# Attention with the value products two units behind, two buffers for the turned probabilities, and the next unit's maxima between a unit's two normalisations

## The reference, cut to what matters

```python
def one_block(qblk):
    s = jnp.einsum('bqhgd,bkhd->bhgqk', qblk, k).astype(jnp.float32) * scale
    p = jax.nn.softmax(s, axis=-1).astype(v.dtype)
    return jnp.einsum('bhgqk,bkhd->bqhgd', p, v)
```

## Time and profile before

| what | value |
|---|---|
| median of 3 runs | 4145.35 us (4144.81 to 4147.48) |
| the profiled execution | 4145.56 us, its trace spans 4143.8 us |
| attention loop in the trace | from scores(0) at 189.85 us to TensorE's restart at 366.76 us |
| mean granted TensorE clock | 0.983 of full speed |

### The profile page before, as it was taken

One profiled execution on the slowest core, in us unless ns is written; L12 is line 12 of the kernel. 1 busy time (PEld: TensorE's weight loads), 2 busy tenths in 40 slices (PEclk: granted clock), 3 DMA queues, 4 the chain that ended last, 5 costly groups with the idle time before them and its releaser, 6 DMA issues.

```text
span 4143.8 us, 57586 instructions
## 1 busy us (share of the span) xinstructions
PE 3886.4 (94%) x21170; PEld 3362.8 (81%) x21170; DVE 2826.8 (68%) x4491; ACT 1696.9 (41%) x2936; POOL 2232.5 (54%) x1240
## 2 busy tenths in 40 slices
PE   7978899999999999999979989999999999999997
PEld 5756898888888888878769989888888888788876
DVE  3774227988875588888863322788887548888886
ACT  3264324556666322222231132455666632222223
POOL 1101234665556677777742323465565667777774
PEclk9999999999999999999999999999999999999998
DMA  5302224778888998898945312477888889988994
GB/s 201 124 1 110 100 99 164 249 269 284 292 299 309 314 307 303 301 314 297 316 147 182 107 57 92 160 243 258 280 300 282 311 312 306 314 295 299 313 316 160
DMA packets 395800, 972.44 MB, mean 235 GB/s; under 512 B 32048, under 2 KB 221232, under 8 KB 381744
## 3 DMA queue, kind: packets, MB, share of 16 engines
q1 hardware_dynamic: 301664, 630.72, 45.2%
q0 software_dynamic: 92160, 335.59, 22.7%
q10 hardware_dynamic: 1744, 3.21, 0.2%
HBM read 835.37 MB, written 133.96 MB: 234 GB/s over the span
## 4 chain that ended last, share of the span: by engine, by line
issue 41%; POOL 34%; PE 17%; DMA 4%; DVE 3%; ACT 1%; POOLq 0%; DVEq 0%; ACTq 0%
POOL SL L444 18%; POOL ROWS L451 14%; PE PS L762 10%; PE PS L564 5%; POOL SL L435 3%; DMA ROWS<-u_exp,EI 2%; DMA ROWS<-v_exp,EI 1%; PE PS L754 1%; DVE ROWS L1267 1%; PE PS L715 1%; DVE OH L1256 0%; DVE PO L1193 0%; ACT SH L995 0%; PE PS L774 0%; DVE TS L1188 0%
## 5 line engine op out<-in xcount | busy, mean ns | idle before, releaser
L444 POOL TENSOR_TENSOR SL<-RW,SH 128x1024 fp32r<-128x1024 f32 x512 | 1284.0, 2508 | 928.6 <-ACT SH L995 887.7
L774 PE MATMUL PS<-WH,SH 128*128 128x480 f32 x2048 | 786.9, 384 | 63.3 <-DVE WL L1317 60.7
L762 PE MATMUL PS<-HH,SH 128*128 128x480 f32 x2048 | 804.5, 393 | 7.8 <-POOL SL L444 6.5
L995 ACT CAST SH<-RW 128x1024 fp32r<-128x1024 f32 x512 | 535.9, 1047 | 613.8 <-PE PS L762 514.1
L762 PE MATMUL PS<-HL,SH 128*128 128x480 f32 x2048 | 780.0, 381 | 0.0
L762 PE MATMUL PS<-HH,SL 128*128 128x480 f32 x2048 | 779.8, 381 | 0.0
L774 PE MATMUL PS<-WH,SL 128*128 128x480 f32 x2048 | 777.2, 379 | 0.0
L774 PE MATMUL PS<-WL,SH 128*128 128x480 f32 x2048 | 776.9, 379 | 0.0
L435 POOL TENSOR_TENSOR SL<-RW,SH 128x1024 fp32r<-128x1024 f32 x84 | 202.5, 2414 | 815.8 <-ACT SH L819 815.8
L1034 ACT CAST WH<-GL 128x480 fp32r<-128x480 f32 x256 | 152.0, 594 | 938.1 <-DVE GL L1311 934.0
L1273 DVE SCALAR_TENSOR_TENSOR ACC<-ROWS,AA,ACC 128x1024 f32<-128x1024 f32 x256 | 399.1, 1559 | 186.8 <-DMA ROWS<-v_exp,EI 174.4
(11 more groups left out here) (171 smaller groups left out, 5358.6 us busy)
## 6 DMA issues: line engine op xcount, KB each, us to landing
RW<-u_blk SPq DMA_DIRECT2D x256, 512.0 KB, 4.3
RW<-v_blk SPq DMA_DIRECT2D x256, 512.0 KB, 5.5
gate_acts<-GE SPq DMA_DIRECT2D x256, 240.0 KB, 2.9
router_weights<-GT SPq DMA_DIRECT2D x60, 1024.0 KB, 4.7
GB<-router_weights SPq DMA_DIRECT2D x32, 1920.0 KB, 12.7
GL<-gate_acts SPq DMA_DIRECT2D x256, 240.0 KB, 4.7
RW<-wstream SPq DMA_DIRECT2D x100, 512.0 KB, 4.5
AW<-wpairs SPq DMA_DIRECT2D x40, 1024.0 KB, 5.2
```

The source lines that it names most:

```text
L444: nc.gpsimd.tensor_tensor(SL[:, r % 2], RW[:, r % RAW], SH[:, r % 2].bitcast(F32), ALU.subtract).then_inc(raw_used, 1)
L762: last = mm(PS[:, n % 2, NG:NS], w[:, n % 2, j], a[:, j, NG:NS], start=(j == 0 and q == 0), stop=(j == DJ - 1 and q == 2))
L774: last = mm(PS[:, dj, NG:NS], w[:, k % 2, dj], a[:, k, NG:NS], start=start, stop=stop)
L995: nc.scalar.copy(SH[:, r % 2], RW[:, r % RAW]).then_inc(hi_done, 1)
```

## The change

Three edits, all in the attention loop:

1. **Order on TensorE and ScalarE.** values runs two units behind instead of one: round n is scores(n+1), values(n-2), turn(n, 0), turn(n, 1). On ScalarE turned(n-1) now stands ahead of out_high(n-2). PT gets a second buffer (in the area WK, which has no other use in this loop), taken in turn.
2. **Order on VectorE.** Round n becomes: normalisation (n, 0), maxima of n+1 (0, 1), normalisation (n, 1), out_low(n-2).
3. RS holds the sums of two units (4 columns instead of 2).

No instruction is added or removed in the loop; only their places and the buffers change.

```diff
-    RS = tiny("RS", 2)
+    RS = tiny("RS", 4)
...
-    PT, _ = sb("PT", [P, 2, NT], F32, at=at_H + 3 * NT * 4)
+    PT = [sb(f"PT{k}", [P, 2, NT], F32, at=at)[0] for k, at in enumerate((at_H + 3 * NT * 4, at_WK))]
...
             if n + 1 < len(UNITS):
                 scores(n + 1)
-            if n > 0:
-                values(n - 1)
+            if n > 1:
+                values(n - 2)
             turn(n, 0)
             turn(n, 1)
+        values(len(UNITS) - 2)
         values(len(UNITS) - 1)
...
+            if n > 0:
+                turned(n - 1)
             if n > 1:
                 out_high(n - 2)
-            if n > 0:
-                turned(n - 1)
+        turned(len(UNITS) - 1)
         out_high(len(UNITS) - 2)
-        turned(len(UNITS) - 1)
         out_high(len(UNITS) - 1)
...
+        def largest(n, half):
+            w = key_tiles(n) * P
+            dve.wait_ge(score_done, 2 * n + half + 1)
+            v.reduce_max(MX[:, half:half + 1], PSf[:, half * 1024:half * 1024 + w], AX_X)
+            dve.drain()
+            v.tensor_scalar(NB[:, half:half + 1], MX[:, half:half + 1], -1.0, None, ALU.mult).then_inc(nb_done, 1)
+
+        def normalised(n, half):
+            dve.wait_ge(exp_done, 2 * n + half + 1)
+            at = 2 * (n % 2) + half
+            v.reciprocal(RI[:, half:half + 1], RS[:, at:at + 1])
+            dve.drain()
+            pr = PR[n % 2][:, half, 0:key_tiles(n) * P]
+            v.tensor_scalar(pr, pr, RI[:, half:half + 1], None, ALU.mult).then_inc(p_done, 1)
+
+        largest(0, 0)
+        largest(0, 1)
         for n in range(len(UNITS)):
-            w = key_tiles(n) * P
-            for half in range(2):
-                dve.wait_ge(score_done, 2 * n + half + 1)
...
+            normalised(n, 0)
+            if n + 1 < len(UNITS):
+                largest(n + 1, 0)
+                largest(n + 1, 1)
+            normalised(n, 1)
             if n > 1:
                 out_low(n - 2)
```

More of the change, by code:

```diff
@@ L685, in values @@
                         val = VC[:, m * P + a:m * P + b]
-                    last = mm(PSf[a:b, 3584:3584 + P], val, PT[:, half, kt * P:(kt + 1) * P],
+                    last = mm(PSf[a:b, 3584:3584 + P], val, PT[n % 2][:, half, kt * P:(kt + 1) * P],
                               start=(kt == 0), stop=(kt == k - 1))
@@ L944, in turned @@
                 act.wait_ge(pt_done, 2 * n + half + 1)
-                nc.scalar.copy(PT[:, half, 0:min(w, NS)],
+                nc.scalar.copy(PT[n % 2][:, half, 0:min(w, NS)],
                                PSf[:, 2048 + half * 512:2048 + half * 512 + min(w, NS)]).then_inc(ptc_done, 1)
             if w > NS:
-                nc.scalar.copy(PT[:, :, NS:NT], PSf[:, 3072:3072 + 2 * P].rearrange("p (h k) -> p h k", h=2)
+                nc.scalar.copy(PT[n % 2][:, :, NS:NT], PSf[:, 3072:3072 + 2 * P].rearrange("p (h k) -> p h k", h=2)
                                ).then_inc(ptc_done, 1)
@@ L957, in _ @@
                 nc.scalar.activation(PR[n % 2][:, half, 0:w], PSf[:, half * 1024:half * 1024 + w], ACT.Exp,
-                                     bias=NB[:, half:half + 1], accum_out=RS[:, half:half + 1]).then_inc(exp_done, 1)
+                                     bias=NB[:, half:half + 1], accum_out=RS[:, 2 * (n % 2) + half:2 * (n % 2) + half + 1]).then_inc(exp_done, 1)
+            if n > 0:
+                turned(n - 1)
             if n > 1:
                 out_high(n - 2)
-            if n > 0:
-                turned(n - 1)
+        turned(len(UNITS) - 1)
         out_high(len(UNITS) - 2)
-        turned(len(UNITS) - 1)
         out_high(len(UNITS) - 1)
@@ L1400, in out_low @@
                             ALU.subtract).then_inc(oh_done, 1)
-        for n in range(len(UNITS)):
-            w = key_tiles(n) * P
-            for half in range(2):
-                dve.wait_ge(score_done, 2 * n + half + 1)
[L1406 to L1415, removed]
+        def largest(n, half):
[13 more added lines that the diff above has]
+        largest(0, 1)
+        for n in range(len(UNITS)):
+            normalised(n, 0)
[3 more added lines that the diff above has]
+            normalised(n, 1)
             if n > 1:
```

## The result

The changed kernel took 4162.02 us (median of 6 runs, 4159.48 to 4166.11), the kernel before 4145.97 beside it; the ratio is 1.0039, with a 95% interval of 1.0027 to 1.0052. That is 16 us slower, above the forecast of +5.9 us and above the range's end of 4159. Slower was forecast, but by +0.14%, less than the 0.2% that I had put as the least to be told from no change.

The account below looks back on a forecast made before the run. The attention loop was taken as bound by a chain of scores, maxima and exponentials (4.37 us a large step). Terms -6.9 + 11.0 + 1.8 = +5.9 on 4145.56 gave 4151.5, less 0.2 for the median 4151.3; range 4147.5 to 4159.

Parts of the forecast that it names:

- Small steps: Seven loop steps of a small unit: no wait for copies, 2.90 against 3.89 us, -0.99 each, -6.9 in all.
- Large steps behind a large unit: 24 loop steps: late second normalisation delays transposes and next scores, 4.83 against 4.37 us, +0.46 each, +11.0 in all.
- Large steps behind a small unit: Seven loop steps: ScalarE's out_high waits for value products of the same step, 4.62 us, +0.25 each, +1.8 in all.
- The end: From scores(39) to TensorE's restart, 8.17 us before: put at no change, within 0.5 us either way.
- The sum at full clock: Total over the attention loop's steps: -6.9 + 11.0 + 1.8 = +5.9 us.
- the fourth rival, the clock: Longer TensorE pause once per group lowers the clock: 1.2 us a step, up to 28 in 24 steps, 4180; chance 0.04.
- Nothing new binds: Rival: large steps stay at 4.37 us and only small steps gain, -6.9 us, 4138.5; chance 0.07.
- Only ScalarE's limit binds: Rival: late transposes cost less, all 31 large steps at 4.62 us, +1.6 us, 4147; chance 0.08.
- The dearer late normalisation: Rival: turn(n, 1) ahead of scores(n+2) in 24 large steps costs 0.61 us each, +10.8 us, 4156; chance 0.13.
- the price of ScalarE's limit: Sum for that rival: 31 x 0.25 - 6.9 = +0.9, about +2.4 with 0.3 a step for rounding; written as +1.6.

Follow-up runs that it names:

- the run with the normalisations first: The changed kernel with both normalisations of n ahead of the maxima of n+1 on VectorE; 4141.41 us, ratio 0.9983.
- the run with the filled pause: The changed kernel plus seven idle matmuls between turn(n, 0) and turn(n, 1) in the round of each group's second unit; 4157.43 us, ratio 1.0022.
- three behind: The changed kernel with out_high and out_low three units behind, and both normalisations ahead of the maxima on VectorE; 4140.22 us, ratio 0.9982.
- the last two kernels: Three behind with the scores by half, 4133.92 us; and the same with one maximum between the normalisations, 4145.25 us.
- scores per half: The kernel before, with scores of half 0 waiting only for its own exponential and issued ahead of half 1; 4137.1 us, ratio 0.9978.
- the kernel three behind with the scores by half: Three behind, with each half's scores waiting only for its own exponential and half 0 issued first; 4133.92 us, ratio 0.9966.

## Why the prediction was wrong

**Small steps:** forecast 2.90, measured 2.93; the gain is 0.96 each, against 0.99 forecast.

**Large steps behind a large unit:** forecast 4.83, measured 4.85. The links are there one by one: the reciprocal directly behind the second NB, the transposes waiting for VectorE, the scores behind them with no wait of their own. That the place of this normalisation is the cause is shown by the run with the normalisations first.

**Large steps behind a small unit:** forecast 4.62, measured 4.52. The value products start at +1.28 when nothing holds them, where I had +1.41 from a row in which they were held for a moment. The exponentials 0.78 apart were right.

**The end:** forecast at no change, measured 8.28 against 8.17.

**The sum at full clock** was thus right: +5.9 forecast, +6.6 measured in the run with the filled pause, +5.6 without the slower start of its trace.

**The step that failed is the fourth rival, the clock.** I named the place (the wait from about +2.4 to +4.2, 1.8 us, once per group, where values belongs to a small unit; measured 1.74) and then gave it a chance of 0.04 and nothing in the sum, with the reason that the clock is 1.00 now with TensorE busy 3.90 of 4.37 us. That row was of the wrong step. The step of the same kind in the kernel before is this one, with the pause of 1.41 us in it:

```profile
281.03:285.40 4.37, 2.96 (x22) 1.96 (x22) 3.48 (x10) 2.25 (x9) 0.00 (x0) 1.00 0.00 0
...
345.47 0.70 PE L657 MATMUL PS<-BIG 64*128 64x512 f32 x2 [1.76 <-ACT PR L957]
```

It has TensorE busy 2.96 of 4.37 us at a clock of 1.00; the changed kernel has 3.12 of 4.85 in its place. So the share there fell only from 0.68 to 0.64, by less than the tenth that I allowed for, and the clock fell behind it all the same. The second row shows that a pause of 1.76 us stood once in the kernel before too, where I had written 1.41 as the longest, and the clock stayed up. What failed is thus the inference from a clock of 1.00 in rows of before to a clock of 1.00 after the change: neither the right row nor the longest pause would have shown that it falls. The runs showed that it does in six of eight groups, in both traces, and not when the pause is filled.

The price was wrong the other way, 28 us for 24 steps: the clock recovers within one step, so a fall costs 1.3 to 1.5 us. The five falls beyond the start cost 6.76 us, and with 2.26 for the slower start (scores(0) to scores(4), 23.46 us against 21.20 in the filled run) that is 9.0 us in all. With 5.9 + 9.0 the forecast would have been 4160.5, in the measured span.

The range ended at 4159 because it left this case out. What stays open is what makes the clock fall. Two groups of eight are spared in each trace, though their pause is the same 1.74 us. The run with the normalisations first had one fall behind a pause of 1.74 us and none behind one of 1.78; three behind had pauses of 1.73 and 1.78 without a fall; and the last two kernels had falls where TensorE had paused for 0.44 us at most in the 6 to 7 us before. So the length of the pause decides nothing alone. Filling it shows, in one trace, only that in the changed kernel the falls do not come without it.

**The other rivals.** Nothing new binds: no; the queues held. Only ScalarE's limit binds: that is the run with the normalisations first, not the change. The dearer late normalisation: no, its links cost what the rows said. In the price of ScalarE's limit one sum of mine does not come out: 0.9 with 0.3 a step for 31 steps is 10.2, and the 2.4 that I wrote goes with 0.05 a step. Nothing in the forecast hangs on it.

## What to carry to other kernels

Ask of each moved instruction what is queued behind the instruction that waits for it: here moving a normalisation behind two maxima that were never late put a wait of 0.87 us for it ahead of the transposes and so of the next scores, +0.48 us on each of 24 steps. Where every large wait is one chain (scores, maxima, exponentials, scores), reordering the work beside the chain gains only at its odd steps; shortening the chain (scores per half) gained 7.3 us, the reordering three behind 4.3, and the two together 11.1. Before splitting such a group of matmuls, ask what they cost apart: the scores of the halves took about twice as long where a wait stood between them. And when a change lengthens TensorE's pauses, look at the one round where the least work meets the longest wait, not at the mean: behind that round the clock fell here. But its rows alone did not tell that it would; filling the pause did.

## What I had not expected of the hardware

A matmul load of no use made the loop faster: 14 more passes in one round of each group took 9.0 us off it, as the granted clock stayed at 1.00. Without them it was 0.50 for some 3 us behind that round in six of eight groups. The same kind of work in the round ahead, 16 passes, did not help.

The clock also fell where TensorE had hardly paused: to 0.61 on average from 293.62 to 297.98 us of the kernel three behind with the scores by half, behind 6.73 us in which it was busy 6.20.

The scores of the two halves share TensorE if both are issued at once: four matmuls, each on 64 partitions, take 1.13 to 1.14 us, and two alone take 1.12. From 210 to 350 us the wide ones take 30.1 us for 106 in the kernel before and 45.1 for 112 with the scores by half.
